# First row tile of x loaded as two half-width transfers, its squares summed in two operations, the first sum entering as the root's addend

## The reference

```python
def rms_norm(x, g, eps=NORM_EPS):
    xf = x.astype(jnp.float32)
    y = xf * lax.rsqrt(jnp.mean(xf * xf, axis=-1, keepdims=True) + eps)
    return (y * g.astype(jnp.float32)).astype(x.dtype)
...
        h = rms_norm(x, pre_mix_g[l])
        z = jnp.einsum('bsd,de->bse', h, w_in[l])
```

## Time and profile before

| | us |
|---|---|
| median of 3 runs | 1089.78 (1089.76 to 1089.88) |
| the profiled execution, whole | 1089.69 |
| its span, first to last instruction | 1087.8 |
| PE busy | 1080.2 (99% of the span) |
| ACT busy | 577.4 (53%) |
| DVE busy | 592.7 (54%) |
| POOL busy | 573.9 (53%) |

### The profile page before, as it was taken

One profiled execution on the slowest core, in us unless ns is written; L12 is line 12 of the kernel. 1 busy time (PEld: TensorE's weight loads), 2 busy tenths in 40 slices (PEclk: granted clock), 3 DMA queues, 4 the chain that ended last, 5 costly groups with the idle time before them and its releaser, 6 DMA issues.

```text
span 1087.8 us, 17431 instructions
## 1 busy us (share of the span) xinstructions
PE 1080.2 (99%) x6776; PEld 964.6 (89%) x6776; DVE 592.7 (54%) x995; ACT 577.4 (53%) x1127; POOL 573.9 (53%) x450
## 2 busy tenths in 40 slices
PE   9999999999999999999999999999999999999998
PEld 7878788999999999888887787889999999988886
DVE  4364544888888884010345535458888888820103
ACT  6656684666555554221457568656565555531212
POOL 3534264567666665544344234645666666654440
PEclk9999999999999999999999999999999999999999
DMA  8423212424433434522343222132443333363212
GB/s 280 140 63 90 77 50 87 155 79 117 116 92 105 117 99 160 188 97 97 89 142 100 77 78 78 64 123 86 117 117 95 101 116 99 97 216 117 96 56 78
DMA packets 144790, 118.32 MB, mean 109 GB/s; under 512 B 3754, under 2 KB 120004, under 8 KB 144708
## 3 DMA queue, kind: packets, MB, share of 16 engines
q1 hardware_dynamic: 144692, 117.20, 34.3%
q10 hardware_dynamic: 16, 0.00, 0.0%
HBM read 110.90 MB, written 6.29 MB: 108 GB/s over the span
## 4 chain that ended last, share of the span: by engine, by line
PE 98%; ACT 1%; DVE 0%; DMA 0%; issue 0%; DVEq 0%; ACTq 0%
PE banks L600 30%; PE banks L602 30%; PE banks L601 30%; PE banks L662 2%; PE banks L690 2%; PE banks L609 1%; PE banks L675 1%; PE banks L866 1%; PE banks L700 1%; DMA x_rows<-in_x_dram 0%; PE banks L707 0%; ACT junk L1079 0%; PE banks L956 0%; DVE silu_t L1773 0%; PE banks L949 0%
## 5 line engine op out<-in xcount | busy, mean ns | idle before, releaser
L531 POOL TENSOR_TENSOR w_lo<-raw,w_hi 128x512 fp32r<-128x512 f32 x204 | 260.4, 1300 | 299.5 <-ACT w_hi L1071 299.5
L549 POOL TENSOR_TENSOR w_lo<-raw,w_hi 128x512 fp32r<-128x512 f32 x200 | 259.8, 1310 | 143.0 <-ACT w_hi L1140 138.4
L600 PE MATMUL banks<-xg_hi,w_hi 128*128 128x256 f32 (+1 forms) x896 | 277.0, 309 | 0.2
L602 PE MATMUL banks<-xg_lo,w_hi 128*128 128x256 f32 (+1 forms) x896 | 274.7, 307 | 0.0
L601 PE MATMUL banks<-xg_hi,w_lo 128*128 128x256 f32 (+1 forms) x896 | 274.5, 306 | 0.0
L1071 ACT ACTIVATE w_hi<-raw 128x1024 fp32r<-128x1024 f32 x102 | 107.0, 1060 | 164.4 <-PE banks L602 155.6
L1140 ACT ACTIVATE w_hi<-raw 128x512 fp32r<-128x512 f32 x200 | 124.9, 630 | 112.2 <-DVE raw L1756 60.7
L600 PEld LDWEIGHTS banks<-xg_hi,w_hi 128*128 128x128 f32 x896 | 171.5, 191 | 9.4 <-issue 2.0
L602 PEld LDWEIGHTS banks<-xg_lo,w_hi 128*128 128x128 f32 x896 | 171.4, 191 | 7.8
L601 PEld LDWEIGHTS banks<-xg_hi,w_lo 128*128 128x128 f32 x896 | 171.6, 191 | 6.9
L600 PE MATMUL banks<-w_hi,hid_hi 128*128 128x512 f32 x352 | 137.3, 390 | 0.0
(11 more groups left out here) (175 smaller groups left out, 1840.5 us busy)
## 6 DMA issues: line engine op xcount, KB each, us to landing
raw<-in_w_gate_up_dram SPq DMA_DIRECT2D x88, 512.0 KB, 4.0
raw<-in_w_down_dram SPq DMA_DIRECT2D x44, 512.0 KB, 3.6
raw<-in_w_in_dram SPq DMA_DIRECT2D x40, 512.0 KB, 3.8
raw<-in_w_out_dram SPq DMA_DIRECT2D x16, 512.0 KB, 3.5
x_spill<-x_rows SPq DMA_DIRECT2D x8, 512.0 KB, 4.7
x_rows<-x_spill SPq DMA_DIRECT2D x8, 512.0 KB, 4.8
x_rows<-in_x_dram SPq DMA_DIRECT2D x4, 512.0 KB, 6.9
out_dram<-x_rows SPq DMA_DIRECT2D x8, 256.0 KB, 2.0
```

Of the source, the lines that this page charges most:

```text
L531: last = tt(lo[:, piece], raw_half(l, c, h)[:, piece], hi[:, piece].bitcast(F32), ALU.subtract)
L549: tt(lo, full, hi.bitcast(F32), ALU.subtract).then_inc(w_ready, 1)
L600: mm(o, stat[0], mov[0], start=first, stop=False)
L602: return mm(o, stat[0], mov[1], start=False, stop=last)
```

## The change

The load of x tile 0 becomes two loads of 512 columns each, 256 KB, with a semaphore of its own for the first (`x0_landed`); the second keeps `x_landed[0]`. They are issued one behind the other ahead of all other loads. On ACT the one `Square` over 1024 columns becomes two over 512, each waiting for its half. DVE forms `first_bias` = first sum / 1024 + 1e-6 in one small operation, and the root takes the second sum as its input and `first_bias` as the addend, where it took the whole sum and a constant. The other three row tiles and all later groups are as they were. Three semaphores and two small tiles (128x2 and 128x1) are added.

```diff
+        first_ssq = sb("first_ssq", [P, 2])
+        first_bias = sb("first_bias", [P, 1])
...
-            load_x(0)
+
+            sp.dma_start(x_rows[:, 0, 0:HALF], x_view[0][:, 0:HALF]).then_inc(x0_landed, 16)
+            sp.dma_start(x_rows[:, 0, HALF:D], x_view[0][:, HALF:D]).then_inc(x_landed[0], 16)
             load_half(0, 0, 0)
             load_x(1)
...
+            def root_of_first_row():
+                act.wait_ge(x0_landed, 16)
+                fn(junk[:, 0:HALF], x_rows[:, 0, 0:HALF], ACT.Square, accum_out=first_ssq[:, 0:1]).then_inc(first_ssq_ready, 1)
+                act.wait_ge(x_landed[0], 16)
+                fn(junk[:, HALF:D], x_rows[:, 0, HALF:D], ACT.Square, accum_out=first_ssq[:, 1:2]).then_inc(ssq_x_ready, 1)
+                act.wait_ge(first_bias_ready, 1)
+                act.wait_ge(ssq_x_ready, 1)
+                fn(root_x[:, 0:1], first_ssq[:, 1:2], ACT.Sqrt, scale=1.0 / D, bias=first_bias[:, :])\
+                    .then_inc(root_x_ready, 1)
...
             for r in range(ST):
-                act.wait_ge(x_landed[r], 16)
-                root_of_row(0, r)
+                if r == 0:
+                    root_of_first_row()
+                else:
+                    act.wait_ge(x_landed[r], 16)
+                    root_of_row(0, r)
...
+            dve.wait_ge(first_ssq_ready, 1)
+            ts(first_bias[:, :], first_ssq[:, 0:1], 1.0 / D, EPS, ALU.mult, ALU.add).then_inc(first_bias_ready, 1)
             dve.wait_ge(gain0_ready, 1)
             norm_row(0, 0)
```

More of the change, by code:

```diff
@@ L181, in trunk @@
         x_spill = nc.dram_tensor("x_spill", [S, D], F32)
+        x0_landed = sem("x0_landed")
+        first_ssq_ready = sem("first_ssq_ready")
+        first_bias_ready = sem("first_bias_ready")
         x_landed = [sem(f"x_landed{r}") for r in range(ST)]
```

## The result

| | before | changed |
|---|---|---|
| median, us (22 runs each) | 1089.84 | 1091.10 |
| lowest to highest, us | 1089.59 to 1090.29 | 1089.75 to 1092.82 |
| ratio | | 1.0013, 95% interval 1.0007 to 1.0019 |
| profiled execution, us | 1089.69 | 1090.21 |
| its span, us | 1087.8 | 1088.4 |

The changed kernel is 1.26 us slower, about 0.13%. The executions also spread over 3.1 us, where those of before spread over 0.7. The profiled execution is one of the mildest, the second lowest of 22: it shows 0.5 us of the 1.3.

The account below looks back on a forecast made before the run. PE was taken to bound the kernel from about 12 us on. Saving 0.41 in the squares, less 0.10 for the split and 0.01 for PE's third pass, gives 0.30 us: forecast 1089.48, range 1089.0 to 1090.2.

Parts of the forecast that it names:

- What bounds the kernel: PE, from about 12 us on: whatever moves the begin of its unbroken run moves the end by as much.
- The landing of the halves: Row tile 0's transfers at the start: first half lands near 3.70 us, the second near 4.45.
- Rival C: Transfer start-up at row tile 0 is paid twice, shifting all behind by 2.3 us: 1091.7 to 1092.1; chance 0.03.
- The squares and the addend: ACT and DVE on tile 0: root at about 5.26 instead of 5.57, saving 0.31 us, the addend hidden.
- e: Extra delay of row tile 0's second half from splitting the load: taken as 0.10 us, between 0 and 0.47.
- The step that failed: First weight half at ACT: data not there before 5.68 plus 0.10, so its operation starts at 5.80, not 5.77.
- rival B: The late first weight half becomes the bound, through ACT, POOL and PE's third pass: 1089.9 to 1090.4; chance 0.12.
- point of decision: Weight half's delay from which it sets tile 1's turning: 0.37 us, from 0.09 landing margin and 0.28 PE idle.
- still have 0.2 us to spare: Row tile 1 at ACT: landing at 7.35 leaves its squares 0.2 us of margin even when they start 0.3 earlier.
- no change: Whole time against the kernel before: a difference within 0.2%, or 2.2 us, can't be told; chance 0.96.

Follow-up runs that it names:

- e5: Changed kernel with the second column half of row tile 0 issued by ACT behind its load of the gains: 1091.88 us, +2.05 against the kernel before.
- g1: Kernel before with the first weight half issued ahead of the whole row tile 0: 1091.93 us, +2.06 against the kernel before.
- g2: Changed kernel with the first weight half issued ahead of both halves of row tile 0: 1091.60 us, +1.73 against the kernel before.
- e1: Changed kernel's two loads of row tile 0, but one square waiting for both, as in the kernel before: 1091.27 us, +1.44 against the kernel before.
- e2: Changed kernel's two squares and addend, but one whole load of row tile 0 ahead of both: 1089.94 us, +0.11 against the kernel before.
- f1: Kernel before with an unused 4 KB transfer issued between the whole row tile 0 and the first weight half: 1090.64 us, +0.78.
- h1: Kernel before with SP waiting for the identity matrix before issuing the first weight half, no transfer added: 1089.87 us, -0.02.
- f4: Kernel before with row tile 1 loaded in two column halves instead of tile 0, its one square waiting for both: 1089.73 us, -0.13.
- g4: Changed kernel with PE running the first weight half's third pass behind the turning of tile 1: 1092.08 us, +2.21 against the kernel before.
- h2: Kernel before with the first weight half loaded in two transfers of 256 KB behind the whole row tile 0: 1090.23 us, +0.34.
- f2: Changed kernel with row tile 1 and all later issues held until row tile 0's first half has landed: 1090.15 us, +0.29 against the kernel before.
- e3: Kernel before with row tile 0 loaded in two transfers of 64 full rows each, one square: 1091.26 us, +1.43.
- h3: Changed kernel with row tile 1 and all later issues held until the gains are placed: 1090.74 us, +0.85 against the kernel before.

## Why the prediction was wrong

**What bounds the kernel: right.** PE's run is unbroken from about 12 us on, and what moves its begin moves the end; 0.40 and 0.18 us at the start are the 0.6 of the span. What the prediction left out is that a longer wait at the start can also bring the lower clock (e5, g1, g2).

**The landing of the halves: right where it counts.** Forecast 3.70 and 4.46; they landed near 3.4 and 4.42. The second is within 0.04. The first is 0.3 early, so that half the bytes did not cost half the time; as the first square was hidden anyway, this changed nothing.

**Rival C didn't happen.** The halves landed 1.0 us apart, not 2.3. The Trainium skill ("DMA: Bandwidth & Descriptors", the section on the anatomy of one DMA) gives a fixed cost of about 2.0 us for a DMA, fitted on transfers that GpSimd issued. That it is paid again between queued transfers isn't seen here. The page puts most of it down to waiting for the receipt; that it then overlaps is a conclusion of the prediction, which only the landings bear out.

**The squares and the addend: right.** Forecast root at 5.26, measured 5.26. That it fits to 0.01 is luck: e was 0.06 instead of 0.10, and from the second square to the root it took 0.82 instead of 0.78. The addend was computed from 4.15 on, far ahead. g2 against g1 shows a gain of 0.33 us (0.0 to 0.8) in the whole time where the weights are out of the way.

**The step that failed** was this one: "But the data isn't there before 5.68 + e. So this operation starts at 5.80 instead of 5.77." I took the delay of the weight half to be the same e = 0.10 as that of row tile 0's second half, since bytes and not issues time a queued transfer. For the second half that held. For the weight half it was 1.19 us in the profiled run, and, to judge by their times, more in most of the others. The mechanism is that of rival B, to which I gave 0.12: the first weight half becomes the bound. Its point of decision, a delay of 0.37 us, was well placed, and by it the turning should start 1.19 - 0.37 = 0.82 later; in the chain it starts at 11.33 instead of 10.49, 0.84. Half of this is taken back at once, since DVE's second half is ready by then and the eight transposes take 0.87 instead of 1.31. B's size was wrong: I let the delay reach twice an issue of SP, 0.94 us, which gives 0.94 - 0.37 = 0.57, and put B at 1090.4 at most. It also had the whole transfer late, and not one engine's part of it. The median is 1091.10, so my range, 1089.0 to 1090.2, missed it.

A second step of the same kind failed: the squares of row tile 1 "still have 0.2 us to spare". The tile landed at 8.25, not at 7.35 + e, so that they could not have started at 7.7 even with the weights in time; from 8.27 on they would have been 0.3 later than before.

**What stands behind the delay.** Shown: it comes from the load and not from the squares (e1, e2); a transfer of 4 KB ahead of the weights, with row tile 0 whole, brings 0.78 of it (f1), so that the smaller pieces of row tile 0 aren't needed for the greater part; a later issue without a transfer doesn't move the median, though some runs with it are late (h1); the same split behind the weights costs nothing (f4), and with the weights first the change gains (g2 against g1). So an added transfer at the head of the queue makes the transfers behind it late, often and by far more than its bytes. The operand with the smallest margin is behind it (0.09 at ACT, 0.28 at PE). The landings by engine say in what form: the median part of the weights lands at 5.51 instead of 5.44, the last at 6.86 instead of 5.68. Row tile 1 lands late in the same way (8.2 in the changed kernel and g4, 8.46 in h2), and in e1 it was row tile 0's second half.

That a late weight half costs time as it did here shows in seven profiles, whose chain goes through it, ACT, POOL and PE's third pass to the turning of tile 1:

| | weight half landed | turning of tile 1 starts | time above the profiled run before |
|---|---|---|---|
| e2 | 6.21 | 10.69 | 0.18 |
| f2 | 6.66 | 11.14 | 0.55 |
| changed | 6.87 | 11.33 | 0.52 |
| h1 | 7.00 | 11.47 | 0.82 |
| f1 | 7.14 | 11.60 | 0.95 |
| e3 | 7.24 | 11.71 | 1.02 |
| h3 | 7.31 | 11.77 | 1.05 |

The turning starts 4.46 to 4.48 us behind the landing in each. f1 and h3 are here with their median runs.

**Open** is why single DMA engines fall behind by over 1 us when the head of the queue has one transfer more, whether two equal halves really cost more than a whole and 4 KB (1.26, 1.0 to 1.7, against 0.78, 0.6 to 1.4: the intervals overlap), how much the later issue adds, and why holding back the later issues to 3.4 us took away 0.95 (f2). Only one profile exists for each kernel, and the landing varies from run to run. That the late engine explains each single execution's time is argued from the profiled ones and the spread, not shown for the others: the changed kernel's median of 1091.10 is above all seven in the table. In its longest runs the clock may have a part. The five slowest of the 22 (1092.04 and more) all have a mean granted clock of 0.998, of the other 17 only two have that and the rest more; none of the five was profiled.

**The chances.** I named 0.2% as what can be told from no change. The before runs spread over 0.7 us, 0.06%, and with 22 runs each a loss of 0.13% was plain. By the 0.2% it is still "no change", to which I gave 0.96; that came true without the mechanism behind it, and so by luck. No version here beats the kernel before clearly; f4, at -0.13 us, is at the edge.

## What to carry to other kernels

Ahead of a split, look not only at the transfer that is split, but at the one behind it, and read its margin: here the weight half had 0.09 us at ACT and lost 1.2. A transfer is landed when its slowest part is, so a queue whose bytes arrive on time on average can still deliver an operand late; take the next operand's landing with a range of its own, a microsecond wide at the start of a kernel. And a pass that sits in an idle gap of the bounding engine is free only there: moved out of it, it costs its full time. Where a variant lets the matrix engine run idle at the start, read the granted clock before its time is put down to the transfer alone.

## What the runs showed of the hardware

- The first weight half, 512 KB in one transfer and second or third in the queue, landed between 5.6 and 7.3 us in these profiles; its median part landed between 5.2 and 5.9 in all but two of them (6.2 in h3, 6.6 in e3).
- The granted clock of TensorE was 1.00 over the start in the kernel before and in the changed one, and fell to 0.50 for a time in e5, g1 and g2, after PE had been idle for 2.0 to 2.7 us. Eight transposes at the lower level took 1.97 us (e5) and 1.96 (g2), against 1.10 before.
- A transfer on ACT's queue beside a full SP queue took 4.8 us for 256 KB; as second on SP's queue the same bytes took 3.2.
- 64 rows of 4 KB (256 KB) landed at 4.36 us as the first transfer, no earlier than the 512 KB of the kernel before, whereas 128 rows of 2 KB landed near 3.4. At the head of the queue the bytes alone don't tell the landing.
- SP's own issues can take longer: in the changed kernel, where landings were late, that of row tile 2 took 1.28 us instead of 0.47. Which is the cause of which isn't shown:

```profile
3.62 1.28 SPq L462 DMA_DIRECT2D x_rows<-in_x_dram  x1
```
